# One layer of a hybrid attention encoder with grouped experts on one NeuronCore: scores left negated, with their minimum as the exponent's shift

## Chip, core and metric

The kernel runs on one core of a Trainium2 chip. The metric is the device time of one execution in microseconds. Three executions of the kernel before took 1049.94 to 1052.03 us, with a median of 1051.31.

## The reference

One step of a one-layer encoder over 1024 prompt tokens and 32 sample tokens, width 1024, all in float32:

```python
h = rmsnorm(x); z = h @ w_in              # -> qA | kA | vA | qB | kB | vB
# mixer A: 8 query heads, 2 kv heads, window of own chunk + 2 before, learned sinks
s = where(valid, q @ k.T / 8, -1e30)
m = maximum(max(s), sink)
e = exp(s - m); p = e / (sum(e) + exp(sink - m))
# mixer B: 8 heads, own chunk + 8 before, learned bias by distance
s = where(valid, q @ k.T / 8 + rel_bias, -1e30)
p = softmax(s)                            # the same, without a sink
out = p @ v
x = x + w_out @ concat(rmsnorm(out_A), rmsnorm(out_B))
x = x + HierMoE(rmsnorm(x))               # top 1 of 4 groups, then top 2 of 8 experts
```

For this case the two lines with `m` and `e` matter: the greatest score of a row is subtracted ahead of the exponent.

## The kernel before

The tokens are laid in nine tiles of 128 rows (eight of the prompt, one of the sample). The program of each engine is written out by hand, with semaphores between engines; each engine works through its own list in order. There are four stages:

- projection with w_in and norms of the heads, about 0 to 294 us;
- attention, output projection and router, interleaved, about 294 to 676 us;
- the choice of experts and the tables of slots, to about 731 us;
- 24 steps of experts' matmuls with gathered rows, to the end. The expert weights stream in over the sync engine's queue; those of experts 1 to 4 wait for the last pair of attention heads, those from expert 5 on for the slot tables.

**The attention stage.** A *unit* u is one head of one mixer on one tile t of queries: 16 units for each tile, 144 in all, handled in pairs v (units 2v and 2v+1). A unit has 128 query rows and, as its width, 128 to 640 key columns: up to 256 in mixer A, up to 640 in mixer B. A unit goes through the engines like this:

1. TensorE makes the scores (`scores`, matmul at L1351) in PSUM.
2. VectorE adds the mask or the bias and takes the row's maximum in one instruction, `tensor_tensor_reduce` in `biased` (L1036). The trace shows it as two: CUSTOM_DVE_ANT_0, which writes the biased scores to `sp`, and DVE_READ_ACCUMULATOR2_ANT, which writes the maximum to a column of `mx`. For mixer A the maximum starts from the sink. Then L1040 multiplies this column by -1 into a column of `negm`, after a wait on VectorE's own semaphore (`link`), and raises `s_sp`.
3. ScalarE takes the exponent in place with `negm` as its bias and sums the row (`probs`, L764, in the trace ACTIVATE and ACTIVATION_READ_ACCUMULATOR). For mixer A it also takes the exponent of the sink (L769).
4. TensorE transposes the probabilities (`transpose_probs`, L1366); VectorE (L954) and ScalarE (L750, L753) copy them out of PSUM, a half each.
5. TensorE multiplies with the values for both units of a pair (`values`, L1383); ScalarE copies the result (`pair_out`, L730), TensorE transposes it back (`pair_back`, L1396), and VectorE divides by the sums (`divide`, L966, L967 or L969, then L973).

In the loop over v, TensorE's list is: transposes of unit 2v-2, scores of pair v+1, a piece of other work, the transposing back of pair v-3, transposes of unit 2v-1, another piece, values of pair v-2. ScalarE's is: copy out pair v-3, copy of unit 2v-2, exponent of unit 2v+2, pieces, copy of 2v-1, exponent of 2v+3, pieces. VectorE's is: copy of unit 2v-2, `biased` of 2v+2, pieces, division of pair v-3, copy of 2v-1, `biased` of 2v+3, pieces.

The *pieces* belong to the tile before and the one before that: squares of the mixer outputs (ScalarE L776) and their norm (VectorE L983), transposes (TensorE L1412), output projection (TensorE L1438), residual (VectorE L999), squares of the residual (ScalarE L791) with its reciprocal root (L644, L645), the second norm (VectorE L1006), its transposes (TensorE L1450, ScalarE L795, VectorE L1009) and the router (TensorE L1458, L1466; VectorE L1016, L1020). ScalarE's L784 copies the first half of the L1412 transposes. For the first tiles, for which there is no such work yet, TensorE runs filler matmuls in their place (`keep_busy`, L1251).

All of SBUF is one tensor, `arena`, cut up by `place(n)` in order, n floats for each partition. `negm` (two tiles by 16 columns) and then `mx` stand ahead of `psum_e` and all the large buffers.

Of the kernel before, what the change touches and what calls it, by code (L numbers as in the profile page):

```python
# [22 lines left out]
ALU = mybir.AluOpType  # L23
ACT = mybir.ActivationFunctionType
# [9 lines left out]
HEADS = 8  # L34
# [23 lines left out]
class Chain:  # L58
# [12 lines left out]
    def link(self, ins):  # L71
        ins.then_inc(self.sem, 1)
        self.k += 1
        v = self.base + self.k
        v = v if self.i is None else self.i * self.per + v
        self.eng.wait_ge(self.sem, v)
# [27 lines left out]
def build(nc, d, o):  # L104
    ctx = ExitStack()
    with ctx:
        def sem(name):
            return ctx.enter_context(nc.semaphore(name))

        arena = ctx.enter_context(nc.sbuf_tensor("arena", [P, ARENA], F32))  # L110
        ps = ctx.enter_context(nc.psum_tensor("ps", [P, 8 * 512], F32))
        top = [0]

        def place(n, at=None):
            a = top[0] if at is None else at
            if at is None:
                top[0] += n
            assert a + n <= ARENA, (a, n)
            return arena[:, a:a + n]
# [8 lines left out]
        sinks = place(HEADS)  # L128
# [4 lines left out]
        eps = place(1)  # L133
        ss26, rs26 = place(26), place(26)
        negm = place(2 * 16).rearrange("p (b c) -> p b c", b=2)
        mx = place(2)
        psum_e = place(2 * 16).rearrange("p (b c) -> p b c", b=2)
        esink = place(HEADS)
        rden = place(16)
# [30 lines left out]
        sp = place(4 * KW).rearrange("p (b c) -> p b c", b=4)  # L170
# [82 lines left out]
        def scores_at(m, r, width):  # L253

            if m == 0:
                return (640, 1024)[r]
            return 0 if r == 0 else 2048 - max(width, 512)
# [37 lines left out]
        s_sp = sem("scores_biased")  # L295
# [93 lines left out]
        def unit_info(u):  # L389

            t, m, h = units[u]
            segs = tile_keys(t)[m]
            tiles, c = [], 0
            for col, n in segs:
                for k in range(0, n, P):
                    tiles.append((c + k, (col + k) // P, min(P, n - k)))
                c += n
            return t, m, h, segs, tiles, c

        def stat_at(m, h):  # L400

            return h // 4 * 8 + m * 4 + h % 4
# [6 lines left out]
        def pt_of(u):  # L409
            _, m, h = units[u]  # L410
            return (pt_a, pt_b)[m][:, h % 2]

        def first_bias(t, m):

            if t == NT - 1:
                return 0 if m == 0 else 2 * P
            return ((1 - min(t, 1)) if m == 0 else (4 - min(t, 4))) * P
# [202 lines left out]
        def _(act):  # L620
# [111 lines left out]
            def copy_pt(u):  # L732

                if not 0 <= u < NU:
                    return
                _, _, _, _, tiles, _ = unit_info(u)
                cut = (len(tiles) + 1) // 2
                act.wait_ge(s_pt, u + 1)
                rest = tiles[cut:]
                if not rest:  # L740
                    act.sem_inc(s_pta, 1)
                    return
                if u >= 4:
                    act.wait_ge(s_pv[u % 2], u // 2 - 1)
                c0 = 0
                full = [x for x in rest if x[2] == P]
                ins = None
                if full:
                    c0 = len(full) * P
                    ins = nc.scalar.activation(pt_of(u)[:, cut * P:cut * P + c0], bank(5, 0, c0), ACT.Copy)  # L750
                if len(full) < len(rest):
                    n = rest[-1][2]
                    ins = nc.scalar.activation(pt_of(u)[0:n, cut * P + c0:cut * P + c0 + P], bank(5, c0, c0 + P)[0:n], ACT.Copy)  # L753
                ins.then_inc(s_pta, 1)

            def probs(u):

                if u >= NU:
                    return
                t, m, h, segs, tiles, width = unit_info(u)  # L760
                act.wait_ge(s_sp, u + 1)
                c = stat_at(m, h)
                shift = negm[:, t % 2, c:c + 1]
                nc.scalar.activation(sp[:, u % 4, 0:width], sp[:, u % 4, 0:width], ACT.Exp,  # L764
                                     bias=shift, accum_out=psum_e[:, t % 2, c:c + 1]).then_inc(s_p, 1)
                if m == 0:
                    if t >= 1:
                        act.wait_ge(s_on, u // 2 - 7)
                    nc.scalar.activation(esink[:, h:h + 1], sinks[:, h:h + 1], ACT.Exp, bias=shift).then_inc(s_es, 1)  # L769
# [11 lines left out]
            def act_pieces(t, g):  # L781
# [11 lines left out]
                if g == 21:  # L793
                    act.wait_ge(s_t2, 2 * t + 1)
                    nc.scalar.activation(h2t[:, 0:4], bank(6).rearrange("p (g c) -> p g c", g=4), ACT.Copy).then_inc(s_h2a, 1)  # L795

            probs(0)
            probs(1)
            for v in range(NV + 3):
                pair_out(v - 3)  # L800
                copy_pt(2 * v - 2)
                probs(2 * v + 2)
                if v % 8 == 3 and v >= 8:
                    squares_out(v // 8 - 1)
                pieces(act_pieces, 2 * v)
                copy_pt(2 * v - 1)
                probs(2 * v + 3)
                pieces(act_pieces, 2 * v + 1)
# [68 lines left out]
        def _(dve):  # L877
            chain = Chain(dve, s_dve)
            link = chain.link
# [142 lines left out]
            def biased(u):  # L1022

                if u >= NU:
                    return
                t, m, h, segs, tiles, width = unit_info(u)
                c = stat_at(m, h)
                if t == 0 and m == 1:
                    dve.wait_ge(s_bm, h + 1)
                dve.wait_ge(s_qk[u % 2], u // 2 + 1)  # L1030
                if u >= 4:
                    dve.wait_ge(s_pt, u - 3)
                b0 = first_bias(t, m)
                at = scores_at(m, u % 2, width)
                add = bm[:, h, b0:b0 + width] if m else maska[:, b0:b0 + width]
                link(nc.vector.tensor_tensor_reduce(  # L1036
                    out=sp[:, u % 4, 0:width], in0=ps[:, at:at + width], in1=add, scale=1.0,
                    scalar=sinks[:, h:h + 1] if m == 0 else -3e38, op0=ALU.add, op1=ALU.max,
                    accum_out=mx[:, u % 2:u % 2 + 1]))
                nc.vector.tensor_scalar(negm[:, t % 2, c:c + 1], mx[:, u % 2:u % 2 + 1], -1.0, None,  # L1040
                                        ALU.mult).then_inc(s_sp, 1)

            biased(0)
            biased(1)
            for v in range(NV + 3):
                copy_pt(2 * v - 2)
                biased(2 * v + 2)
                pieces(dve_pieces, 2 * v)
                divide(v - 3)
                copy_pt(2 * v - 1)  # L1050
                biased(2 * v + 3)
                if v % 8 == 3 and v >= 8:
                    norm_out(v // 8 - 1)
                pieces(dve_pieces, 2 * v + 1)
# [186 lines left out]
        def _(pe):  # L1241
# [82 lines left out]
            def scores(v):  # L1324
                if v >= NV:
                    return
                t, m, h, segs, _, width = unit_info(2 * v)
                if v >= 1:
                    wide = unit_info(2 * v - 1 if m == 0 else 2 * v)[5] > 512
                    if wide or v >= 2:  # L1330
                        pe.wait_ge(s_sp, 2 * v if wide else 2 * v - 2)
                p = h // 2
                runs = []
                c = 0
                for col, n in segs:
                    for k0, k1 in ((0, min(n, 512)), (512, n)):
                        if k0 < k1:
                            runs.append((c + k0, k1 - k0, col + k0))
                    c += n
                for i in range(len(runs)):  # L1340
                    for r in range(2):
                        a = r * HD
                        if r == 1 and width > 512:
                            c, step, col = ((P, 512, segs[0][0] + P), (0, P, segs[0][0]))[i]
                        else:
                            c, step, col = runs[i]
                        at = scores_at(m, r, width) + c
                        assert at // 512 == (at + step - 1) // 512
                        q = qt[a:a + HD, t, 4 * m + p, :]
                        kt = kta[a:a + HD] if m == 0 else ktb[a:a + HD, p]  # L1350
                        ins = mm(ps[:, at:at + step], q, kt[:, col:col + step], start=True, stop=True)  # L1351
                        if i == len(runs) - 1:
                            ins.then_inc(s_qk[r], 1)
# [351 lines left out]
```

## Time and profile before

| | |
|---|---|
| median of three runs | 1051.31 us (1049.94 to 1052.03) |
| the profiled execution | 1051.28 us, its span 1049.5 us |
| TensorE matmul | 974.7 us busy, 93% |
| TensorE weight load | 505.4 us, 48% |
| VectorE | 404.4 us, 39% |
| ScalarE | 306.5 us, 29% |
| GpSimd | 89.2 us, 9% |
| granted clock of TensorE, mean | 0.974 |

The span reaches from the first to the last instruction. Busy shares are means over stages that have different limits: in the attention stage VectorE and ScalarE are busy for over half the time and the DMA engines hardly at all, in the expert stage DMA is. The matmuls are pipelined and their ends are modelled, so a busy TensorE need not be at its peak. A wait in the trace names the instruction that ended it.

### The profile page before, as it was taken

What the parts mean: (1) busy time and instruction counts of PE and PEld (TensorE: products, weight loads), DVE (VectorE), ACT (ScalarE), POOL (GpSimd) and SP (SyncE); (2) the same over time, 40 slices, a digit from 0 to 9 for tenths busy, and PEclk for the clock granted to TensorE, in tenths of its full rate; (3) what the DMA queues carried; (4) which work ended last, traced back from release to release, by engine and by line L of the source; (5) the groups of instructions that cost most, each with busy time, mean ns of one, the idle gap of its engine ahead of it and who ended that gap; (6) DMA issues with size and microseconds to landing.
All of it is one profiled execution on the core that took longest, in us unless ns stands there. A gap on an engine that the chain in (4) does not pass through costs nothing. (4 is left out here: it accounts for less than half of the span.)

```text
span 1049.5 us, 16397 instructions
## 1 busy us (share of the span) xinstructions
PE 974.7 (93%) x6173; PEld 505.4 (48%) x6173; DVE 404.4 (39%) x1227; ACT 306.5 (29%) x920; POOL 89.2 (9%) x72
## 2 busy tenths in 40 slices
PE   6999999999988898989889899989999999988995
PEld 3444555455465454555555556568443333323331
DVE  0343233432566466475656646257231111111110
ACT  1221222212445455464554545120111111111110
POOL 1000000000110000000000000000122222222111
PEclk9999999999999999999999998998999999999998
DMA  8510111101271101010110401291599999999972
GB/s 349 207 40 1 40 40 40 40 0 41 101 295 53 60 3 61 1 62 21 41 61 2 177 5 62 75 423 66 204 309 376 393 386 386 391 383 392 371 279 41
DMA packets 34440, 164.65 MB, mean 157 GB/s; under 512 B 7808, under 2 KB 9888, under 8 KB 20928
## 3 DMA queue, kind: packets, MB, share of 16 engines
q1 hardware_dynamic: 24192, 134.92, 32.4%
q0 software_dynamic: 6912, 17.32, 6.7%
q10 hardware_dynamic: 3264, 11.44, 2.7%
q8 instruction: 47, 0.77, 0.3%
q14 instruction: 25, 0.20, 0.1%
HBM read 147.10 MB, written 24.41 MB: 163 GB/s over the span
## 5 line engine op out<-in xcount | busy, mean ns | idle before, releaser
L1264 PE MATMUL ps<-arena 128*128 128x512 f32 (+1 forms) x640 | 251.0, 552 | 9.7 <-DMA arena<-in_w_in 9.7
L1264 PEld LDWEIGHTS ps<-arena 128*128 128x128 f32 x640 | 121.0, 190 | 134.5 <-issue 128.7
L1530 PE MATMUL ps<-arena 128*32 128x512 f32 x1536 | 173.6, 603 | 9.0 <-DMA arena<-in_wexp 7.6
L764 ACT ACTIVATE arena<-arena 128x256 f32<-128x256 f32 (+6 forms) x144 | 83.9, 582 | 128.3 <-DVE arena L1040 128.1
L1438 PE MATMUL ps<-arena 128*128 128x512 f32 x256 | 121.0, 605 | 0.0
L1530 PEld LDWEIGHTS ps<-arena 128*32 128x32 f32 x1536 | 50.3, 111 | 114.7 <-issue 112.7
L1036 DVE CUSTOM_DVE_ANT_0 arena<-ps,arena 128x256 f32<-128x256 f32 (+6 forms) x144 | 78.0, 541 | 31.4 <-PE ps L1351 31.2
L1548 PE MATMUL ps<-arena 128*32 128x512 f32 x768 | 87.2, 592 | 0.6 <-ACT arena L853 0.6
L1202 DVE SCALAR_TENSOR_TENSOR arena<-ps,arena 128x256 f32<-128x256 f32 x24 | 11.6, 484 | 172.5 <-ACT arena L845 172.5
L1366 PE MATMUL ps<-arena 128*128 128x128 f32 (+1 forms) x400 | 73.1, 288 | 5.4 <-ACT arena L750 2.0
L954 DVE COPY arena<-ps 128x128 f32<-128x128 f32 (+2 forms) x144 | 52.9, 367 | 46.5 <-PE ps L1366 46.0
L683 ACT ACTIVATE arena<-ps,arena 128x512 f32<-128x512 f32 (+1 forms) x36 | 24.7, 687 | 156.6 <-PE ps L1264 155.6
L894 DVE TENSOR_TENSOR arena<-arena 128x640 f32<-128x640 f32 (+1 forms) x18 | 18.5, 1026 | 132.3 <-ACT arena L681 79.4
L1438 PEld LDWEIGHTS ps<-arena 128*128 128x128 f32 x256 | 44.6, 189 | 46.9 <-issue 44.3
L1351 PE MATMUL ps<-arena 64*128 64x256 f32 (+4 forms) x384 | 63.9, 432 | 1.1 <-DVE arena L1040 0.7
L560 POOL DMA_INDIRECT arena<-h_rows,arena x24 | 26.1, 1087 | 456.2 <-DVE arena L1169 438.3
L1383 PE MATMUL ps<-arena 128*64 128x128 f32 (+1 forms) x800 | 63.2, 288 | 0.0
L845 ACT ACTIVATE arena<-ps 128x256 f32<-128x256 f32 x24 | 9.2, 383 | 170.5 <-PE ps L1530 170.5
L1366 PEld LDWEIGHTS ps<-arena 128*128 128x128 f32 (+1 forms) x400 | 44.6, 142 | 28.3 <-issue 25.9
L571 POOL DMA_INDIRECT out_y<-arena x24 | 38.0, 1582 | 226.3 <-issue 164.1
L1383 PEld LDWEIGHTS ps<-arena 128*64 128x64 f32 (+1 forms) x800 | 44.3, 140 | 22.9 <-issue 21.5
L1251 PE MATMUL ps<-arena 128*128 128x128 f32 x400 | 54.9, 295 | 0.0
(161 smaller groups left out, 895.2 us busy)
## 6 DMA issues: line engine op xcount, KB each, us to landing
arena<-in_wexp SPq DMA_DIRECT2D x96, 1024.0 KB, 23.4
arena<-in_x SPq DMA_DIRECT2D x18, 512.0 KB, 4.3
arena<-in_w_in ACTq DMA_DIRECT2D x3, 2048.0 KB, 23.0
arena<-in_xT SPq DMA_DIRECT2D x9, 512.0 KB, 3.5
arena<-in_w_out SPq DMA_DIRECT2D x1, 4096.0 KB, 13.9
out_y<-arena SPq DMA_DIRECT2D x8, 512.0 KB, 2.6
h_rows<-arena SPq DMA_DIRECT2D x8, 512.0 KB, 2.9
arena<-in_bias SPq DMA_DIRECT2D x1, 2560.0 KB, 9.0
```

The lines of the kernel that those rows point to most:

```text
L571: pool.indirect_dma_start(out=o["y"], out_offset=bass.IndirectOffsetOnAxis(ap=slot_token[:, s:s + 1], axis=0), in_=yb[:, s % 3], in_offset ...
L764: nc.scalar.activation(sp[:, u % 4, 0:width], sp[:, u % 4, 0:width], ACT.Exp, bias=shift, accum_out=psum_e[:, t % 2, c:c + 1]).then_inc(s_ ...
L954: nc.vector.tensor_copy(pt_of(u)[:, 0:cut * P], bank(4, 0, cut * P)).then_inc(s_ptv, 1)
L1036: link(nc.vector.tensor_tensor_reduce(out=sp[:, u % 4, 0:width], in0=ps[:, at:at + width], in1=add, scale=1.0, scalar=sinks[:, h:h + 1] if ...
L1251: mm(bank(b, 0, P), ident, ident, start=True, stop=True)
L1264: ins = mm(bank(Z_BANK[c], 0, CHUNK[c]), xt[:, j, k, :], w_in[:, a:a + CHUNK[c]], start=(k == 0), stop=(k == KD - 1))
L1351: ins = mm(ps[:, at:at + step], q, kt[:, col:col + step], start=True, stop=True)
L1366: ins = nc.tensor.transpose(dst[0:n], sp[:, u % 4, c:c + n], ident)
L1383: ins = mm(pv_ps[r * HD:(r + 1) * HD], kv, pt_of(2 * v + r)[0:n, i * P:i * P + P], start=(i == 0), stop=(i == len(tiles) - 1), tile_positi ...
L1438: ins = mm(bank(6), ot[:, c], w_out[:, c, 512 * n:512 * n + 512], start=(c == 0), stop=(c == KD - 1))
L1530: ins = mm(bank(s % 2)[u:u + UNIT], xgt[:, s % 2, k, u:u + UNIT], ring[expert_of(s, q) % RING][:, k * 512:(k + 1) * 512], start=(k == 0), ...
L1548: ins = mm(bank(5 + n)[u:u + UNIT], hdt[:, s % 2, f, u:u + UNIT], ring[expert_of(s, q) % RING][:, a:a + 512], start=(f == 0), stop=(f == 1 ...
```

## The change

VectorE's reduction now multiplies the sum of score and bias by -1 as it writes it, and keeps the running minimum, starting from the negated sink in mixer A. That minimum is the negative of the maximum, so it goes straight to the column of `negm`, and L1040 and `mx` are gone. `s_sp` is raised by the reduction itself. ScalarE's exponent takes scale -1 with the same bias. The negated sinks, `nsinks`, eight columns in the place of the two of `mx`, are made once, by one instruction ahead of the first unit; this moves all that is placed behind by 24 bytes in each partition.

```diff
-        mx = place(2)
+        nsinks = place(HEADS)
...
-                nc.scalar.activation(sp[:, u % 4, 0:width], sp[:, u % 4, 0:width], ACT.Exp,
+                nc.scalar.activation(sp[:, u % 4, 0:width], sp[:, u % 4, 0:width], ACT.Exp, scale=-1.0,
                                      bias=shift, accum_out=psum_e[:, t % 2, c:c + 1]).then_inc(s_p, 1)
...
-                link(nc.vector.tensor_tensor_reduce(
-                    out=sp[:, u % 4, 0:width], in0=ps[:, at:at + width], in1=add, scale=1.0,
-                    scalar=sinks[:, h:h + 1] if m == 0 else -3e38, op0=ALU.add, op1=ALU.max,
-                    accum_out=mx[:, u % 2:u % 2 + 1]))
-                nc.vector.tensor_scalar(negm[:, t % 2, c:c + 1], mx[:, u % 2:u % 2 + 1], -1.0, None,
-                                        ALU.mult).then_inc(s_sp, 1)
-
+                nc.vector.tensor_tensor_reduce(
+                    out=sp[:, u % 4, 0:width], in0=ps[:, at:at + width], in1=add, scale=-1.0,
+                    scalar=nsinks[:, h:h + 1] if m == 0 else 3e38, op0=ALU.add, op1=ALU.min,
+                    accum_out=negm[:, t % 2, c:c + 1]).then_inc(s_sp, 1)
+
+            link(nc.vector.tensor_scalar(nsinks, sinks, -1.0, None, ALU.mult))
             biased(0)
             biased(1)
```

## Rows read from the trace of the kernel before

**Rows 1.** Windows: stretch, length, busy time of each engine, TensorE's clock, DMA share, GB/s.

```profile
448.40:494.85 46.45, 42.39 (x293) 25.41 (x291) 27.71 (x94) 23.63 (x76) 0.00 (x0) 1.00 0.10 35
494.85:541.30 46.45, 42.39 (x293) 25.41 (x290) 27.71 (x94) 23.64 (x76) 0.00 (x0) 1.00 0.10 35
...
730.00:1049.00 319.00, 296.95 (x2627) 113.56 (x2626) 54.22 (x104) 44.67 (x96) 64.05 (x48) 0.97 0.87 322
```

**Rows 2.** Waits, 294 to 665 us: total us, times, longest.

```profile
ACT arena L764 <- DVE arena L1040: 128.1, 114, 3.4
...
PE ps L1396 <- ACT arena L730: 15.5, 17, 1.8
...
PE ps L1450 <- ACT arena L795: 2.9, 4, 0.7
```

**Rows 3.** Groups by line: busy us, mean ns | idle before.

```profile
L1036 DVE CUSTOM_DVE_ANT_0 arena<-ps,arena 128x256 f32<-128x256 f32 (+6 forms) x144 | 78.0, 541 | 31.4 <-PE ps L1351 31.2
...
L1040 DVE TENSOR_SCALAR arena<-arena 128x1 f32<-128x1 f32 x144 | 22.1, 154 | 5.0
```

**Rows 4.** Timeline, 494.5 to 497.6 us: start, length, instruction [idle before].

```profile
494.57 0.08 DVE L1036 DVE_READ_ACCUMULATOR2_ANT arena<- 128x1 f32 x1
494.69 0.15 DVE L1040 TENSOR_SCALAR arena<-arena 128x1 f32<-128x1 f32 x1
494.88 0.51 ACT L764 ACTIVATE arena<-arena 128x256 f32<-128x256 f32 x1 [1.50 <-DVE arena L1040]
...
497.27 0.15 DVE L1040 TENSOR_SCALAR arena<-arena 128x1 f32<-128x1 f32 x1
...
497.38 1.28 DVE L1006 SCALAR_TENSOR_TENSOR arena<-arena 128x1024 f32<-128x1024 f32 x1
...
497.48 0.33 PE L1396 MATMUL ps<-arena 128*128 128x128 f32 x1 [1.11 <-ACT arena L730]
```

**Rows 5.** Timeline, 500.1 to 502 us.

```profile
500.31 0.15 DVE L1040 TENSOR_SCALAR arena<-arena 128x1 f32<-128x1 f32 x1
...
500.52 0.70 PE L1351 MATMUL ps<-arena 64*128 64x256 f32 x4 [0.17 <-DVE arena L1040]
...
501.95 0.33 PE L1450 MATMUL ps<-arena 128*128 128x128 f32 x1 [0.73 <-ACT arena L795]
```

**Rows 6.** Timeline, 508.3 to 512.4 us, and the same wait in the last tile.

```profile
508.54 0.15 DVE L1040 TENSOR_SCALAR arena<-arena 128x1 f32<-128x1 f32 x1
508.61 0.18 DVE L1020 TENSOR_TENSOR arena<-ps,arena 128x36 f32<-128x36 f32 x1
...
508.94 0.63 PE L1412 MATMUL ps<-arena 128*128 128x128 f32 x4 [0.28 <-DVE arena L1020]
...
510.62 0.83 ACT L764 ACTIVATE arena<-arena 128x640 f32<-128x640 f32 x1 [0.70 <-DVE arena L1040]
...
512.24 0.33 PE L1396 MATMUL ps<-arena 128*128 128x128 f32 x1 [0.90 <-ACT arena L730]
...
651.19 0.33 PE L1396 MATMUL ps<-arena 128*128 128x128 f32 x1 [0.26 <-ACT arena L730]
```

**Rows 7.** TensorE's waits, 294 to 340 us.

```profile
PE ps L1366 <- ACT arena L750: 1.9, 2, 1.7
PE ps L1396 <- ACT arena L730: 1.2, 3, 0.6
PE ps L1366 <- ACT arena L764: 1.1, 1, 1.1
PE ps L1366 <- DVE arena L954: 0.3, 1, 0.3
```

**Rows 8.** Timeline of VectorE: the first unit's reduction.

```profile
296.11 0.35 DVE L1036 CUSTOM_DVE_ANT_0 arena<-ps,arena 128x128 f32<-128x128 f32 x1 [1.86 <-PE ps L1351]
```

**Rows 9.** Windows: two stretches at the lower clock.

```profile
363.40:370.40 7.00, 6.76 (x41) 4.75 (x43) 4.08 (x18) 3.92 (x13) 0.00 (x0) 0.54 0.42 151
...
636.20:646.40 10.20, 9.92 (x62) 6.87 (x61) 6.71 (x23) 5.49 (x21) 0.00 (x0) 0.50 0.30 103
```

## Prediction

> **What bounds the kernel now.** I read the windows first, then TensorE's waits, then the timeline around each wait. The change touches only the attention stage, 294 to 660 us. In its second half that stage repeats with a period of 46.45 us (one query tile) at full clock, with the same busy times [rows 1]. In one period TensorE is busy for 42.39 us, so it stands for 4.06 us; VectorE is busy for 27.71 and ScalarE for 23.64. TensorE's work sets the pace, and a shorter VectorE pays only where TensorE stands. The reader should not be led by the longest line of [rows 2]: ScalarE waits 128.1 us for the product with -1, but ScalarE has half its time free. What counts is the 15.5 us, in 17 pieces, that TensorE waits at L1396 for ScalarE's copy L730, and the 2.9 us at L1450.
>
> **What the change does.** It removes 144 products of 154 ns, 22.1 us of VectorE [rows 3], and the wait of each on VectorE's own semaphore. It adds one product of 8 columns before the first unit. The reduction keeps its shape (one product by a scale, one addition, one running comparison), with min for max; the exponent is called with scale -1. Eight columns in the place of two also move every buffer behind negm by 24 bytes.
>
> *The price of one product.* [rows 4] show both prices. The accumulator is read at 494.57 us, the product starts at 494.69, ScalarE's exponent at 494.88. The read ends at 494.65 and the product started 0.04 after that, across the semaphore. If the exponent follows the read with the same 0.04, it starts at 494.69: **0.19 us** for whoever waits for the shift. For VectorE's own next instruction the gain is smaller: behind the product at 497.27 the next one started at 497.38, before the product had ended. So **0.11 us** for VectorE's queue. Beside it stands a rule of the Trainium skill, VectorE: DVE Perf Modes, section "The DRAIN you can't avoid": a semaphore between chained VectorE instructions costs nothing on top. By that rule 0.11 is all; if the removed wait did cost its 0.04, the queue would gain 0.15 and the sum below would be about 0.7 us larger. I keep 0.11, which is a row.
>
> *Where a wait holds it.* The period has five waits of TensorE that I followed back to the TensorE instruction that began their chain.
> - First L1396, wait 1.11 us, at 497.48 [rows 4]. Behind it ScalarE runs without a gap from the exponent at 494.88, through the squares and the reciprocal root, to the copy. That exponent waited for one product: 0.19. Seven tiles have it: 7 x 0.19 = **1.3 us**.
> - The scores L1351, wait 0.17 at 500.52, and L1450, wait 0.73 at 501.95 [rows 5]. VectorE's queue from L1006 (497.38) to the reduction before 500.31 is full, so two products lie on this chain: 0.11 at 497.27 and 0.19 at 500.31. Of these 0.30, 0.19 was taken already by the first wait, as TensorE comes earlier. New is 0.11, in the four full-width periods: **0.4 us**.
> - L1412, wait 0.28 at 508.94, and the second L1396, wait 0.90 at 512.24 [rows 6]. The product at 508.54 delays L1020 by 0.07 to 0.11; then VectorE is full up to the product before the exponent at 510.62. Together 0.11 + 0.19 = 0.30. Six tiles have it; the last tile's wait, at 651.19, is only 0.26 [rows 6] and goes whole: 6 x 0.30 + 0.26 = **2.1 us**.
> - The start of the stage, where filler matmuls keep TensorE busy [rows 7]: 1.1 us at L1366 behind the first exponent gives 0.19; the 0.3 behind L954 ends a queue with three products, 0.33, of which 0.19 is taken already, so 0.14; three waits at L1396, 1.2 us together, lie behind a full VectorE queue and give 0.30 each, 0.9; the 1.7 at L1366 behind L750 gives 0.19, and the second wait there its 0.17. Together **1.6 us**.
>
> The rest gives nothing. The other 100 or so products are hidden behind TensorE: of the exponent's waits most end before TensorE asks for the result. L1458 waits for L1009 (VectorE's copy after L1450), whose chain from L1450 holds no product. The new product of the negated sinks falls into 1.86 us in which VectorE waits for the first scores [rows 8]; without that cover it would cost its 0.15. Scale -1 changes no shape on ScalarE: 0. The shift of 24 bytes: the buffers began 12 bytes past a multiple of 64 and now begin 36 past, off both times; I take 0. Its bound is what the expert stage could lose with DMA at 0.87 and TensorE at 296.95 of 319 us [rows 1]; 0.2% of that is 0.6 us either way.
>
> The sum is 1.3 + 0.4 + 2.1 + 1.6 = **5.4 us**. The expert stage begins when routing is done, and routing when attention is done, its weight loads too (the first wait for the last pair of heads), so it moves as a whole. The profiled execution took 1051.28 us (span 1049.5), the median of the runs is 1051.31, so they need no correction: 1051.3 - 5.4 = **1045.9 us**. What is late next is TensorE itself: after the change each period still stands for about 3.5 us, mainly in the same waits.
>
> *Bounds of the two prices.* Low: ScalarE gains only 0.11 like VectorE's queue, and VectorE nothing: 7 x 0.11 twice, and 1.0 at the start, 2.5 us in all. High: 0.19 for both: 7 x 0.19 + 4 x 0.19 + 6 x 0.38 + 0.26 + 2.0 = 6.6 us.
>
> **The rivals.**
> 1. *The clock gives more.* Right behind the longest of L1396's waits, 1.8 us [rows 2], the granted clock is 0.54 from 363.4 to 370.4 us, and from 636.2 to 646.4 it is 0.50, which is 1.2 GHz [rows 9]; in the regular periods, with a wait of 1.11, it stayed at 1.00. The change shortens exactly those waits. TensorE is busy 9.92 + 6.76 us there; at 2.4 GHz this is at most half, 8.3 us less, and perhaps half of that reaches the end, since VectorE and ScalarE do not get faster. If half of these stretches vanish, 2.1 us more: 1043.8, and down to 1041.7 if both do. Against it: shifted by a few us, a fall may also come where there was none. Chance 0.20.
> 2. *The shift is not handed over earlier.* The accumulator's value could reach ScalarE only after what the product's time hid. Then only VectorE's shares stay, 0.11 in 4 + 6 chains and five times at the start: 1.7 us, 1049.6, no change that can be told. Against it: the product itself, which reads that value, started 0.04 after the read's end. Chance 0.09.
> 3. *Slower: the min form of the reduction takes longer.* The trace has only the max form, mean 541 ns, 78.0 us in all [rows 3]. The chains above hold about 7 + 8 + 13 + 9 = 37 reductions. It breaks even at 5.4 / 37 = 0.15 us more for each, and is slower by over 2.1 us from 0.20 us on. At half the rate (some 0.4 us more) the kernel would lose 37 x 0.4 - 5.4 = 9.4 us: 1060.7. Against it: the same number of operations for each element. Chance 0.03.
> 4. *Much faster: the chain through the three engines sets every pair's pace.* Then all 72 pairs of units gain 0.30: 21.6 us, 1029.7. Against it: the 4.06 us of a period that TensorE stands are nearly used up by the five waits above (3.2 us) and the one at L1458, so there is no such chain elsewhere. The Trainium skill speaks for this rival: Perfetto Trace Analysis, section "Identifying the Most-Contended Engine", calls the busy share of matmuls a bad measure of how near TensorE is to its limit. Chance 0.02.
>
> **How the numbers follow.** My forecast has 0.66 (1044.7 to 1048.8 by the bounds of the two prices), the rivals 0.20, 0.09, 0.03 and 0.02. A measurement of this kernel tells a change from none from about 0.2%, 2.1 us. Faster by more: 0.66 + 0.20 + 0.02, less 0.01 for low prices, 0.87. Within it: 0.10. Slower: 0.03. The range leaves out rivals 2 to 4 and the far end of rival 1: 1041.7 to 1048.8.
>
> **What would show it.** The reduction at 541 ns as before; the exponent 0.04 us behind the accumulator's read; a period of about 45.85 us instead of 46.45; the first L1396 wait near 0.9 and the second near 0.7; TensorE's total wait at L1396 down from 15.5 to about 12. I am wrong if the period stays at 46.45, if the reduction's mean rises by 0.15 us, or if most of a difference lies outside the attention stage or in stretches at the lower clock.

## The result, and the profile after

The changed kernel took 1043.56 us, the median of four runs (1042.44 to 1044.11), against 1050.62 (1049.93 to 1052.03) for the kernel before in the same session: 7.1 us less, a ratio of 0.993 with a 95% interval of 0.9913 to 0.9947. In a second session it was 1041.97 us against 1050.34, 0.9924 (0.9905 to 0.9944): 8.4 us less. The direction and the range held; the forecast of 5.4 us was low in both. The first time lies below 1044.7 us, the end of the forecast's own band, and is inside the range only because the range was widened for a rival, the clock.

Profiled, the changed kernel took 1042.44 us with a span of 1040.6, against 1051.28 and 1049.5. Its lines behind L1041 stand one lower than before: L1395, L1449, L1411 and L1365 are L1396, L1450, L1412 and L1366 of [rows 2 to 7].

The windows, two periods of the attention stage, answer to [rows 1]:

```profile
444.59:490.31 45.72, 42.33 (x290) 25.36 (x290) 25.31 (x79) 23.81 (x78) 0.00 (x0) 1.00 0.10 36
490.31:536.02 45.71, 42.33 (x290) 25.36 (x290) 25.30 (x79) 23.80 (x78) 0.00 (x0) 1.00 0.10 35
```

The period fell from 46.44 to 45.71 us, by 0.73. TensorE's work in it is the same (42.33 against 42.39); VectorE's fell by 2.4 us, of which TensorE's timeline received 0.73. In all, VectorE lost 21.4 us of busy time and the kernel 7 or 8.

The waits between 293 and 660 us (total, times, longest) answer to [rows 2], the group of the reduction to [rows 3]:

```profile
ACT arena L764 <- DVE arena L1036: 108.6, 110, 2.2
...
PE ps L1395 <- ACT arena L730: 13.2, 15, 1.6
...
PE ps L1449 <- ACT arena L795: 3.4, 5, 0.7
```

```profile
L1036 DVE CUSTOM_DVE_ANT_0 arena<-ps,arena 128x256 f32<-128x256 f32 (+6 forms) x144 | 78.1, 544 | 29.8 <-PE ps L1350 29.4
```

ScalarE's long wait is shorter by 19.5 us. TensorE's wait at the back transpose fell from 15.5 us in 17 pieces to 13.2 in 15. The reduction in its min form takes 544 ns, in its max form 541.

The timeline around the first of the waits answers to [rows 4]:

```profile
487.72 0.08 DVE L1036 DVE_READ_ACCUMULATOR2_ANT arena<- 128x1 f32 x1
487.84 0.51 ACT L764 ACTIVATE arena<-arena 128x256 f32<-128x256 f32 x1 [1.32 <-DVE arena L1036]
...
490.31 0.08 DVE L1036 DVE_READ_ACCUMULATOR2_ANT arena<- 128x1 f32 x1
490.31 1.28 DVE L1006 SCALAR_TENSOR_TENSOR arena<-arena 128x1024 f32<-128x1024 f32 x1
...
490.45 0.33 PE L1395 MATMUL ps<-arena 128*128 128x128 f32 x1 [0.92 <-ACT arena L730]
...
494.69 0.66 PE L1449 MATMUL ps<-arena 128*128 128x128 f32 x4 [0.73 <-ACT arena L795]
```

The exponent starts 0.12 us behind the start of the accumulator's read, 0.04 behind its end; before it was 0.31 behind the start. That is the 0.19 of the forecast to the hundredth. The next rows hold what was not forecast: VectorE's L1006 starts at the same time as the read, at 490.31, where before it followed 0.22 behind it. The wait at L1395 is 0.92, from 1.11; the one at L1449 is 0.73 as before.

The second group of waits answers to [rows 6]:

```profile
500.69 0.71 PE L1365 MATMUL ps<-arena 128*128 128x128 f32 x5
...
501.16 0.08 DVE L1036 DVE_READ_ACCUMULATOR2_ANT arena<- 128x1 f32 x1
501.16 0.19 DVE L1020 TENSOR_TENSOR arena<-ps,arena 128x36 f32<-128x36 f32 x1
...
501.54 0.29 DVE L973 TENSOR_TENSOR arena<-ps,arena 128x128 f32<-128x128 f32 x1
...
503.07 0.83 ACT L764 ACTIVATE arena<-arena 128x640 f32<-128x640 f32 x1 [0.60 <-DVE arena L1036]
...
504.69 0.33 PE L1395 MATMUL ps<-arena 128*128 128x128 f32 x1 [0.90 <-ACT arena L730]
```

L1412's wait of 0.28 is down to 0.09, less than the 0.15 us from which the views show a wait. The wait of 0.90 at the second back transpose is there unchanged: counted from L1458, ScalarE's chain came earlier by 0.29, and so did TensorE.

### The profile page after: what moved, and what is told of

The parts are those of the page before. It is cut to its first block and busy times, and to the rows that moved or that the text cites. A ratio compares the mean times of both kernels' runs of the same rounds, so it can differ in the third digit from the quotient of the medians.

```text
span 1040.6 us, 16254 instructions
## 1 busy us (share of the span) xinstructions
PE 970.9 (93%) x6173; PEld 500.3 (48%) x6173; DVE 383.0 (37%) x1084; ACT 307.5 (30%) x920; POOL 89.2 (9%) x72
## 5 line engine op out<-in xcount | busy, mean ns | idle before, releaser
L764 ACT ACTIVATE arena<-arena 128x256 f32<-128x256 f32 (+6 forms) x144 | 84.0, 583 | 109.5 <-DVE arena L1036 108.6
L1365 PE MATMUL ps<-arena 128*128 128x128 f32 (+1 forms) x400 | 72.6, 287 | 4.6 <-ACT arena L750 1.5
L1365 PEld LDWEIGHTS ps<-arena 128*128 128x128 f32 (+1 forms) x400 | 44.6, 141 | 27.2 <-issue 25.5
L1382 PEld LDWEIGHTS ps<-arena 128*64 128x64 f32 (+1 forms) x800 | 44.1, 139 | 22.7 <-issue 21.4
```

The costliest lines, as they stand in the source:

```text
L1365: ins = nc.tensor.transpose(dst[0:n], sp[:, u % 4, c:c + n], ident)
L1382: ins = mm(pv_ps[r * HD:(r + 1) * HD], kv, pt_of(2 * v + r)[0:n, i * P:i * P + P], start=(i == 0), stop=(i == len(tiles) - 1), tile_positi ...
```

## Experiments

In the table, the period is the distance of two starts of L1006 in neighbouring tiles, in the part of the stage that repeats and at full clock. The ratio is to the kernel before on the same chip.

| kernel | median us | ratio (95%) | period us |
|---|---|---|---|
| before_again | 1049.88 | 0.9991 (0.998 to 1.0002) | 46.44 |
| after_again | 1041.97 | 0.9924 (0.9905 to 0.9944) | 45.71 |
| min_kept | 1049.6 | 0.9986 (0.9969 to 1.0003) | 46.43 |
| shift_24_bytes | 1051.06 | 1.0009 (0.9997 to 1.0021) | 46.42 |
| own_wait | 1044.88 | 0.9949 (0.9931 to 0.9968) | 46.02 |
| dead_product | 1044.0 | 0.9945 (0.9925 to 0.9964) | 45.79 |
| wait_and_dead | 1045.46 | 0.9946 (0.9929 to 0.9963) | 46.05 |
| two_products | 1059.56 | 1.0085 (1.0061 to 1.0108) | 47.27 |
| early_copies | 1038.47 | 0.9885 (0.9865 to 0.9906) | 44.75 |
| early_copies2 | 1041.05 | 0.9904 (0.9884 to 0.9923) | 44.71 |
| early_copies3 | 1037.76 | 0.9875 (0.9854 to 0.9897) | 44.48 |
| early2_on_before | 1052.49 | 1.0011 (0.9997 to 1.0024) | 45.49 |

The median scatters with the clock by 1 or 2 us, and intervals of neighbouring kernels overlap. The period repeats to 0.02 us in every profile of one kernel; so the fine splits below rest on it.

**The two kernels once more.** Nothing was edited.

> The kernel before once more, unchanged, to see how its stretches at the lower clock and its stage starts scatter between executions. If the excess over the forecast (7.1 us of gain against 5.4) is in the chain, this profile again has a period of 46.45 us in the second half of attention and VectorE's next instruction 0.18 to 0.23 us behind the accumulator's read. If the excess is the clock, the stretch at 0.5 clock ahead of the first scores (291 us) or those behind L1396 move or vanish here, and the spans of two executions of the same kernel differ by 2 us or so.

> The changed kernel once more, unchanged. Chain theory: the period is 45.71 us again, 0.73 below the kernel before, and the gain is 7.1 us within 1. Clock theory: the stretches at 0.5 clock lie elsewhere, and the span changes by 2 us against the first profile of the same kernel while the period does not.

Of the kernel before, a period and a stretch at the lower clock:

```profile
495.11:541.54 46.43, 42.38 (x290) 25.38 (x290) 27.72 (x95) 23.64 (x78) 0.00 (x0) 1.00 0.09 35
635.00:641.80 6.80, 6.56 (x41) 4.66 (x43) 3.73 (x17) 3.95 (x14) 0.00 (x0) 0.50 0.46 154
```

Of the changed kernel, a period and the stretch from the last tile's norm on:

```profile
489.80:535.51 45.71, 42.33 (x290) 25.36 (x290) 25.30 (x81) 23.80 (x78) 0.00 (x0) 1.00 0.10 35
626.07:664.71 38.64, 36.10 (x219) 20.84 (x219) 16.98 (x62) 15.77 (x59) 0.00 (x0) 0.91 0.10 38
```

Both periods repeat. This pair also gives the size of the gain at an equal amount of the lower clock: between the first reduction and the last, both profiles spent 13.7 us at 1.2 GHz, though not at the same places, where the first pair had 23.9 and 20.5. From the first reduction to the last, the stage took 359.73 us before and 353.06 after: **6.7 us** come from the chains. The rest of the difference between the spans, 1048.1 and 1039.9, lies outside this stretch: 0.6 us behind it and 1.0 ahead of it, since the first reduction started at 295.29 and at 294.30, behind the same projection program. Over all profiles of this study it starts between 294.1 and 296.8, with no order by kernel.

**The form of the reduction, and the place of the buffers.** min_kept negates and takes the minimum as the change does, and still has the product:

```diff
+        esmin = ss26[:, 0:2]
...
-                nc.vector.tensor_tensor_reduce(
+                link(nc.vector.tensor_tensor_reduce(
...
-                    accum_out=negm[:, t % 2, c:c + 1]).then_inc(s_sp, 1)
+                    accum_out=esmin[:, u % 2:u % 2 + 1]))
+                nc.vector.tensor_scalar(negm[:, t % 2, c:c + 1], esmin[:, u % 2:u % 2 + 1], 1.0, None,
+                                        ALU.mult).then_inc(s_sp, 1)
```

> The scores are negated and the running minimum taken as in the change, but a product (with 1) still copies the minimum to negm behind the own semaphore. If the gain comes from the missing product alone, this is as the kernel before: within 1 us of it, L1036 at 541 to 544 ns. If the min form or scale -1 in the exponent has a price or a gain of its own (rival 3), it shows here: 37 times the difference of one reduction. If the move of the buffers by 24 bytes matters, this kernel has it too and shows it in the expert stage.

shift_24_bytes is the kernel before with `mx = place(8)`.

> The kernel before with 8 columns for mx in the place of 2: all large buffers lie 24 bytes further, as after the change, and nothing else. Expected 0 within 0.6 us. If the place of the buffers has a part in the excess, it shows as up to 2 us, outside the attention stage.

A period of each, min_kept first:

```profile
449.69:496.12 46.43, 42.35 (x290) 25.36 (x290) 27.74 (x96) 23.68 (x78) 0.00 (x0) 1.00 0.09 35
```

```profile
452.42:498.84 46.42, 42.34 (x290) 25.36 (x290) 27.73 (x95) 23.67 (x78) 0.00 (x0) 1.00 0.10 35
```

46.43 and 46.42 are the kernel before, and both times agree with it within their intervals. The minimum, the scale of -1 in the exponent and the 24 bytes have no price and no gain that a period shows to 0.03 us, or the intervals of the times to 0.3%. The reduction in its min form takes 544 ns in min_kept as well. Rival 3 is out, and the gain comes from the missing product and its wait.

**VectorE's share taken apart.** own_wait is the changed kernel with a wait on the reduction's own semaphore:

```diff
                     accum_out=negm[:, t % 2, c:c + 1]).then_inc(s_sp, 1)
+                dve.wait_ge(s_sp, u + 1)
```

> The changed kernel, but VectorE waits for its own reduction (on the semaphore that ScalarE waits for too) before it goes on; no product. It splits VectorE's share of the price. In the trace of the change the next VectorE instruction starts at the same time as the accumulator's read, where before it started 0.18 to 0.23 us after it; I had forecast 0.11 of gain. If the wait is free, as the rule on chained VectorE instructions has it, this runs as the changed kernel (1043.6). If the wait itself holds the queue, the next instruction starts about 0.12 us behind the read, and some 11 to 17 chain places lose 0.12 each: 1.3 to 2.0 us slower than the change, about 1045.2, period about 45.95 us.

VectorE's timeline, and the period:

```profile
491.63 0.08 DVE L1036 DVE_READ_ACCUMULATOR2_ANT arena<- 128x1 f32 x1
491.75 1.29 DVE L1006 SCALAR_TENSOR_TENSOR arena<-arena 128x1024 f32<-128x1024 f32 x1
```

```profile
445.73:491.75 46.02, 42.26 (x290) 25.36 (x290) 26.02 (x78) 23.83 (x77) 0.00 (x0) 1.00 0.09 35
```

The next instruction now starts 0.12 us behind the read, and the period grows by 0.31, to 46.02. So the wait alone, with nothing to compute, costs almost half of what the change gave, and the time, 1044.88 us, is near the 1045.2 of that case. The rule of the Trainium skill that the forecast set beside its 0.11, that such a wait costs nothing, does not hold here.

dead_product has a product without a wait, into columns that nobody reads:

```diff
+        spare = place(144, at=ARENA - 150)
...
                     accum_out=negm[:, t % 2, c:c + 1]).then_inc(s_sp, 1)
+                nc.vector.tensor_scalar(spare[:, u:u + 1], sinks[:, 0:1], -1.0, None, ALU.mult)
```

> The changed kernel with a product of one column behind each reduction, without a wait, into columns that nobody reads: it costs VectorE's queue but no hand-over to ScalarE. If only the queue's time counts, the loss is what a product's start-to-start takes (0.07 to 0.19 us) at the 11 to 17 places where a full VectorE queue lies on the chain: 1 to 3 us, about 1045.5. The exponent still starts 0.12 us behind the accumulator's read. If the hand-over is what counts (0.19 at some 25 places), the loss here is under 1 us.

```profile
487.40 0.08 DVE L1037 DVE_READ_ACCUMULATOR2_ANT arena<- 128x1 f32 x1
487.40 0.15 DVE L1041 TENSOR_SCALAR arena<-arena 128x1 f32<-128x1 f32 x1
```

```profile
444.27:490.06 45.79, 42.28 (x290) 25.37 (x290) 26.31 (x98) 23.81 (x78) 0.00 (x0) 1.00 0.10 36
```

The product starts together with the read and costs 0.07 us a period. By the medians the loss is 0.4 us against one session of the changed kernel and 2.0 against the other, so the time says little more than that it is small.

wait_and_dead has both lines.

> The changed kernel with both of VectorE's costs given back and the hand-over left short: a wait for its own reduction, then a product into columns that nobody reads. ScalarE's exponent starts 0.12 us behind the accumulator's read, VectorE's next instruction 0.18 to 0.23 behind it as in the kernel before. own_wait cost 0.30 us a period and dead_product 0.07; if they add, the period is 46.09, and the 0.35 left to 46.44 is the hand-over's share alone. If VectorE's queue is all that counts, the period is 46.44 again. Time 1044.5 to 1046.5 in the first case, 1050 in the second.

Its timeline at the first hand-over and ahead of the norm (L1007 is L1006, L765 is L764), and the period:

```profile
491.37 0.09 DVE L1037 DVE_READ_ACCUMULATOR2_ANT arena<- 128x1 f32 x1
...
491.49 0.51 ACT L765 ACTIVATE arena<-arena 128x256 f32<-128x256 f32 x1 [1.31 <-DVE arena L1037]
...
493.96 0.08 DVE L1037 DVE_READ_ACCUMULATOR2_ANT arena<- 128x1 f32 x1
494.08 0.15 DVE L1043 TENSOR_SCALAR arena<-arena 128x1 f32<-128x1 f32 x1
494.18 1.29 DVE L1007 SCALAR_TENSOR_TENSOR arena<-arena 128x1024 f32<-128x1024 f32 x1
```

```profile
448.13:494.18 46.05, 42.26 (x291) 25.36 (x291) 27.74 (x95) 23.81 (x77) 0.00 (x0) 1.00 0.10 36
```

VectorE's norm follows the read by 0.22 us as in the kernel before, the exponent by 0.12 as in the changed one. The period is 46.05: the first of the two cases. The wait and the product together cost 0.34, hardly more than the wait alone, 0.31. What is left to 46.44, **0.39 us** a period, is the hand-over to ScalarE and TensorE alone. The total time agrees (1045.46 in 1044.5 to 1046.5), but it splits less cleanly than the period: this profile had no lower clock behind the last tile's wait.

**Two products.** The kernel before with one more link of the chain:

```diff
+                link(nc.vector.tensor_scalar(mx[:, u % 2:u % 2 + 1], mx[:, u % 2:u % 2 + 1], 1.0, None, ALU.mult))
                 nc.vector.tensor_scalar(negm[:, t % 2, c:c + 1], mx[:, u % 2:u % 2 + 1], -1.0, None,
```

> The kernel before with a second product (with 1) in the chain, again with a wait on the own semaphore. Both prices once more: the exponent 0.19 us later, VectorE's queue 0.19 later. If the price of a product is linear, it costs what the change gave, 7 us: about 1057.7, period about 47.2 us. If TensorE's slack was only just used up before, more waits open and it costs more, 8 to 10 us. If the gain of the change was in part the clock, it costs 5.4.

The timeline of one unit, and three periods:

```profile
578.45 0.08 DVE L1036 DVE_READ_ACCUMULATOR2_ANT arena<- 128x1 f32 x1
...
578.56 0.15 DVE L1040 TENSOR_SCALAR arena<-arena 128x1 f32<-128x1 f32 x1
578.75 0.15 DVE L1041 TENSOR_SCALAR arena<-arena 128x1 f32<-128x1 f32 x1
578.94 0.83 ACT L764 ACTIVATE arena<-arena 128x640 f32<-128x640 f32 x1 [1.62 <-DVE arena L1041]
```

```profile
457.13:505.98 48.85, 44.03 (x290) 26.97 (x290) 30.02 (x112) 23.80 (x77) 0.00 (x0) 0.97 0.09 33
505.98:553.70 47.72, 43.97 (x290) 26.15 (x290) 29.98 (x111) 23.65 (x77) 0.00 (x0) 0.96 0.10 35
553.70:600.97 47.27, 42.44 (x290) 25.37 (x290) 30.01 (x112) 23.81 (x77) 0.00 (x0) 1.00 0.10 34
```

The hand-over is 0.49, from 0.31: the second product, which starts 0.19 behind the first, costs as much as the first. The period at full clock is 47.27, 0.83 above the kernel before. In time it cost 9.4 us by the medians, more than the 7 of a linear price. Part of it is the clock: two of the three periods shown had a granted clock of 0.97 and 0.96 and took 48.85 and 47.72 us, where the kernel before had full clock in these periods. (The profile is of the slowest of its four runs, 1063.65 us, so the median run had less of it.) TensorE's wait at the start of the second and of the third period is the same:

```profile
506.02 0.33 PE L1397 MATMUL ps<-arena 128*128 128x128 f32 x1 [1.24 <-ACT arena L730]
...
553.74 0.33 PE L1397 MATMUL ps<-arena 128*128 128x128 f32 x1 [1.24 <-ACT arena L730]
```

Behind the first the clock fell, behind the second it did not. So the length of this wait alone does not decide it; that the second product brings the lower clock is seen in one profile and not shown further.

**Taking the next waits.** What remained in the changed kernel were waits for ScalarE's copies behind other work in its list. early_copies moves three of them:

```diff
+            def early(v):
+                return 3 <= v < NV and v % 8 in (1, 4)
...
-                pair_out(v - 3)
+                if not early(v - 1):
+                    pair_out(v - 3)
...
                 copy_pt(2 * v - 1)
-                probs(2 * v + 3)
-                pieces(act_pieces, 2 * v + 1)
+                if early(v):
+                    pair_out(v - 2)
+                if v % 8 == 2:
+                    pieces(act_pieces, 2 * v + 1)
+                    probs(2 * v + 3)
+                else:
+                    probs(2 * v + 3)
+                    pieces(act_pieces, 2 * v + 1)
```

> The changed kernel with ScalarE's list put in another order at three places of a tile: pair_out of the pair two behind goes ahead of the exponent (and of the squares L791) where v mod 8 is 1 or 4, and where v mod 8 is 2 the copy L795 goes ahead of the exponent. If TensorE's remaining waits of 0.92 and 0.90 at the back transpose and 0.73 at L1450 are there only because ScalarE works in order, most of 2.5 us a period goes, in 7 tiles some 10 to 16 us: about 1030. If the exponents that are now later by 0.3 to 0.6 us take their place on the chain, under 5 us are gained.

TensorE's greatest wait then (L1376 is the transpose of the probabilities, L750 ScalarE's half of its copy):

```profile
PE ps L1376 <- ACT arena L750: 12.1, 14, 1.5
```

The period fell by 0.96, not by 2.5, and the time was 1038.47 us, not 1030. TensorE passed the back transpose without a wait and stood at the very next thing that it needs from ScalarE, a copy behind the same squares. The forecast for this kernel was wrong by its main term: each wait was priced on its own.

early_copies2 moves that copy too, where v mod 8 is 1 or 4.

> As early_copies, and where v mod 8 is 1 or 4 the copy of the next unit's transposes (copy_pt of 2v) goes ahead of the piece too, since in early_copies TensorE's waits moved to exactly that copy (L750, 0.86 and 0.73 a period, 12.1 us in all). If that copy is the only thing behind the squares and behind L784 that TensorE needs, the period falls from 44.76 by up to 1.6 us to about 43.2, and the time by some 8 to 10 us to about 1029. If the late squares and the late L784 take its place (TensorE's L1450 and L1412 then wait), it falls by under 0.5 us a period, to about 1036.

TensorE's waits (L1462 is L1450 of the kernel before, L1019 is VectorE's norm L1006):

```profile
PE ps L1462 <- DVE arena L1019: 12.6, 7, 2.3
PE ps L1378 <- ACT arena L750: 2.5, 5, 1.5
```

The second case came: 44.71, nothing gained. The squares are later by the two copies, so the norm is, and TensorE waits for it, 1.54 us in the period that I followed. Total time is 1041.05 us, not the 1036 of that case, and no better than early_copies by their intervals; the profiled execution, 1037.15 us, was its fastest.

early_copies3 leaves the squares in their place: `early(v)` is true for v mod 8 = 4 alone.

> The changed kernel with ScalarE's list reordered in two places only: where v mod 8 is 4, pair_out of the next pair ahead of the exponent and copy_pt of the next unit ahead of L784; where v mod 8 is 2, L795 ahead of the exponent. The squares L791 stay where they are, so VectorE's norm L1006 is not made late, on which early_copies2 waited 1.8 us a period. If the waits of 0.90 and 0.73 go for good and the one of 0.92 stays, the period is about 43.9 and the time some 11 us under the changed kernel, about 1031. If they turn up again elsewhere, it is 44.7 as in the other two orders.

```profile
PE ps L1408 <- ACT arena L730: 9.8, 9, 1.6
```

```profile
445.00:489.48 44.48, 42.64 (x290) 25.36 (x290) 25.27 (x81) 24.00 (x78) 0.00 (x0) 1.00 0.10 37
```

44.48, between the two cases; the time, 1037.76 us, missed the 1031 of the first by 7. The wait of 0.92 stayed as expected, those of 0.90 and 0.73 went, and one of 0.24 appeared at the transposes of the probabilities (L1378, behind ScalarE's copy L750). TensorE's busy time in a period rose too, from 42.33 to 42.64 us, for which the runs show no reason. The interval of its ratio, 0.9854 to 0.9897, lies below both intervals of the changed kernel: it is 12.8 us faster than the kernel before and some 5 faster than the change. early_copies can't be told from it.

early2_on_before has the order of early_copies2 in the kernel before.

> The same order of ScalarE's list in the kernel before, with the product kept. The change of this study then acts on another chain: if the product still stands ahead of waits of TensorE, this is slower than early_copies2 by 5 to 7 us. If the new order gives ScalarE and VectorE slack, the product is hidden and the difference is under 2 us.

Two neighbouring periods:

```profile
449.72:495.21 45.49, 42.60 (x290) 25.43 (x290) 27.58 (x95) 23.96 (x77) 0.00 (x0) 1.00 0.10 36
495.21:543.29 48.08, 45.29 (x290) 27.87 (x290) 27.76 (x94) 24.07 (x77) 0.00 (x0) 0.93 0.09 34
```

The product counts for slightly more here, 0.78 us in the one period of this kernel at full clock (45.49 against 44.71), and the kernel is 11 us slower than early_copies2, more than the 5 to 7 of the expectation. The second row shows why: the same work at a mean clock of 0.93 takes 48.08 us, 2.6 more. In all ten runs the mean clock was 0.964 to 0.972, in the four of early_copies2 0.973 to 0.978. So in this order the product goes with more of the lower clock; why it does is open, since the one period at full clock began with a wait of 1.73 us like the two behind it.

## Why the forecast held, and where it was low

- **The number: the direction was right, the place in the range partly luck.** The forecast's own bounds of the two prices ended at 1044.7 us, 6.6 us of gain; 1043.56 and 1041.97 lie below. The lower end of the range, 1041.7, came from rival 1, which was not the cause; the second time is inside by 0.3 us. Of the 2.3 us between 1045.9 and 1043.56, 0.7 are the kernel before, which had a median of 1051.31 in the forecast and 1050.62 beside the change.
- **What bounds the stage: right.** The gain came where TensorE stood and nowhere else. TensorE's work in a period did not change, and its waits shrank at the places that were named.
- **The hand-over, 0.19 us: right**, and the exponent does start 0.04 us behind the end of the read. wait_and_dead measures its part alone, 0.39 a period; by the forecast's terms it was 0.19 at the first wait and 0.19 at the last, 0.38.
- **VectorE's queue, 0.11 us: the term that was too small.** I took the distance from a product to its follower, 0.11, as the product's whole price in the queue, and let the wait ahead of it be free. The measured distance from the read to the next instruction, where that had nothing else to wait for, fell from 0.19 to 0.24 down to 0.00. The wait is the larger part: 0.12 us each time, 0.31 us a period against 0.07 for a product without it. The forecast had 0.22 a period for VectorE and the difference is 0.34. The rule of the Trainium skill (VectorE: DVE Perf Modes, "The DRAIN you can't avoid") that a semaphore between chained instructions costs nothing on top stands against this measurement, and the measurement decides: own_wait paid 0.12 for it. The same section says that a next instruction which is not held starts earlier; with the profile of the change this agrees, where the next instruction starts at the very time of the read.
- **The sum, 5.4 us: low.** With an equal amount of the lower clock the chains gave 6.7. The period gave 0.73 instead of 0.60. In the table, the kernel before and the changed one between the starts of the first seven of VectorE's norms L1006, one a tile (second pair of profiles):

| stretch | before | after | less |
|---|---|---|---|
| first reduction to first L1006 | 65.14 | 64.20 | 0.94 |
| to the second | 43.53 | 41.43 | 2.10 |
| to the third | 44.71 | 44.14 | 0.57 |
| three periods | 139.32 | 137.16 | 2.16 |
| to the seventh | 45.53 | 44.84 | 0.69 |
| to the last reduction | 21.50 | 21.29 | 0.21 |

  The start of the stage, forecast at 1.6 and 0.19 for the first L1396, gave 0.94; the second row gave 2.10, of which the lower clock has a part: the kernel before had 3.4 us of it there, the changed one none. In the first row it is the other way round, 3.4 us in the changed kernel and none in the kernel before. Set beside the first pair of profiles, this allows an estimate: in the first stretch the kernel before took 65.94 us there, with 3.4 us at the lower clock, and 65.14 here without; in the second the changed one took 43.13 there, with 6.4 us of it, and 41.43 here without. At 0.8 to 0.9 us for 3.4, the rows would be some 1.7 and 1.2. Together they gave 3.04, where the forecast had 2.28 (1.79, and 0.30 + 0.19 for the second). How much each owes to the clock was not tried apart.
- **The waits one by one: half right.** The first L1396 came out at 0.92, as forecast. The scores' wait of 0.17 is gone, and from the first L1396 to L1450 behind it the time fell from 4.47 us to 4.24, by 0.23 where 0.11 was forecast: this is the place where a period's gain was larger than the sum, since VectorE's norm and reduction lie on that chain. The second L1396 was forecast near 0.7 and stayed at 0.90, and so L1396's total is 13.2 and not 12: TensorE came earlier by 0.19 at L1412 and by 0.10 at the scores behind it, as much as ScalarE's copy did. VectorE's larger saving did not pass on here, since its division waits for TensorE's own transposes (they end at 501.40 in the timeline above, the division starts at 501.54). From L1458 to the second L1396 the gain was 0.29, the forecast 0.30.
- **Rival 1, the clock:** it moved times by a few us in either direction, but was not the gain's cause. The last tile's stretch at the lower clock stayed in both profiles of the changed kernel, the one near 360 us in one of them. **Rival 2** is out by the exponent's start, **rival 3** by min_kept, **rival 4** by the size, 7 or 8 us and not 21.6.
- **Nothing for the rest: right.** The negated sinks fell into VectorE's wait for the first scores, and the expert stage moved as a whole: the last 389 us had TensorE busy for 358.51 us, before 358.97. From the last reduction to the end the two pairs of profiles took 391.1 and 393.1 us before, 391.4 and 392.5 after.

## What to carry to other kernels

Price a small instruction on a dependent chain three times: its hand-over to whoever waits, its time in its own queue, and the wait that guards it. Here they were 0.19 us, 0.07 and 0.12 each time, and the wait for the engine's own result was worth more than the arithmetic. Then count only the places where the bounding engine stands, and follow each to the instruction that began it: two waits in a row share one gain, and a wait that is removed by reordering can come back, in part or whole, at the next thing that depends on the same list, as three orders of ScalarE's list showed. For differences under 1%, compare a stretch that repeats at full clock; its length was good to 0.02 us where the medians scattered by 1 to 2.

## What was not expected of the hardware

- A VectorE instruction without a wait started at the same recorded time as the accumulator's read ahead of it, some 70 times in one profile; with a wait for its own result, in own_wait, it never started less than 0.12 us behind it.
- TensorE's clock turned small differences of the program into larger ones. The last tile's stretch, from its L1006 to that of the tile behind, took 36.86 us at full clock in own_wait:

```profile
628.87:665.73 36.86, 33.54 (x219) 18.96 (x219) 17.23 (x62) 15.37 (x59) 0.00 (x0) 1.00 0.11 40
```

  against 38.64 us at a mean of 0.91 in after_again above, though own_wait is the slower program by its period. The wait right ahead was the same in both. TensorE's timeline in own_wait, then in after_again:

```profile
629.00 0.33 PE L1397 MATMUL ps<-arena 128*128 128x128 f32 x1 [1.47 <-ACT arena L730]
...
630.21 0.65 PE L1451 MATMUL ps<-arena 128*128 128x128 f32 x4 [0.45 <-DVE arena L1006]
```

```profile
626.26 0.33 PE L1395 MATMUL ps<-arena 128*128 128x128 f32 x1 [1.47 <-ACT arena L730]
...
627.41 1.09 PE L1449 MATMUL ps<-arena 128*128 128x128 f32 x4 [0.40 <-DVE arena L1006]
```

  The same four matmuls took 0.65 us in the one and 1.09 in the other. What of TensorE's work before them decides this, these runs leave open.
- One order of ScalarE's list had 2.6 us more in a period of 45.5 for the clock alone (early2_on_before), more than any edit to the chain in this study was worth in a period.
